# A two-block transformer step in split fp32 on one core: where the second layer's attention units, three norm spreads and the input's transfers stand in the order of work

## The reference, cut to what matters

```python
def rms_norm_2(x, g):
    return x * rsqrt(mean(x * x, axis=-1) + EPS) * g

def first_block(x, c, ...):
    shift, scale, gate = split(silu(c) @ w_mod + b_mod, 3)
    h = rms_norm(x, g_pre) * (1 + scale) + shift
    q, k, v, g_att, u, g_lru, merge = split(h @ w_in)
    ...
    return x + gate * rms_norm(out, g_post)

def second_block(x, c, ctx, ...):
    for l in range(2):
        hx = modulate(rms_norm_2(x, norm1_g[l]), mod_x[0], mod_x[1])
        zx = split(hx @ w_in[l], 10)
        ...
        # y_b: softmax(q1 k1) - lam * softmax(q2 k2), times v, 4 heads,
        #      512 queries over 512 + 256 keys
        x = x + mod_x[2] * (concat([y_a, y_b, y_c, y_d]) @ w_out[l])
        hx = modulate(rms_norm_2(x, norm2_g[l]), mod_x[3], mod_x[4])
        x = x + mod_x[5] * (square(relu(hx @ w1[l])) @ w2[l])
        # l = 0 only: the same for the context
    return rms_norm_2(x, final_g)
```

## Time and profile before

| | |
|---|---|
| median of 3 runs | 2106.29 us (2105.07, 2106.29, 2112.48) |
| profiled execution | 2109.13 us, its span 2107.2 us |
| granted TensorE clock, mean of the span | 0.992 |
| PE busy | 2049.4 us (97%) |
| DVE, ACT, POOL busy | 1271.3, 795.0, 72.4 us |
| DMA | 249.18 MB, mean 118 GB/s |
| largest group | L2005, products of `hxh` with `whi`, 1464 times, 586.4 us |

### The profile page before, as it was taken

The page is one execution under the profiler, slowest core; times in us unless marked ns, Lnnn a source line. Parts: engine busy times, 40 slices in busy tenths (PEclk is TensorE's granted clock), DMA queues, the critical chain, the costliest instruction groups (busy, mean ns, idle before and its releaser), DMA issues.

```text
span 2107.2 us, 26544 instructions
## 1 busy us (share of the span) xinstructions
PE 2049.4 (97%) x11156; PEld 1750.1 (83%) x11156; DVE 1271.3 (60%) x1699; ACT 795.0 (38%) x1126; POOL 72.4 (3%) x81
## 2 busy tenths in 40 slices
PE   6999999999999999999999999999999999999998
PEld 5989888778888988888888888888787788888887
DVE  7467766866757986637446455464687646344343
ACT  4333334584343366434122131122535534132231
POOL 0000000000120000020000000001100010000001
PEclk9999999999999999999999999999999999999999
DMA  8643523524322531123233233232343122222221
GB/s 287 228 157 123 206 94 123 186 98 177 143 100 65 165 98 70 71 92 121 91 110 113 96 134 109 100 120 91 120 148 90 71 90 99 83 99 100 100 98 63
DMA packets 54054, 249.18 MB, mean 118 GB/s; under 512 B 6224, under 2 KB 12512, under 8 KB 35504
## 3 DMA queue, kind: packets, MB, share of 16 engines
q1 hardware_dynamic: 52048, 242.41, 33.3%
q10 hardware_dynamic: 1296, 2.63, 0.4%
q0 software_dynamic: 592, 2.46, 0.3%
HBM read 232.53 MB, written 12.06 MB: 116 GB/s over the span
## 4 chain that ended last, share of the span: by engine, by line
PE 55%; DVE 4%; ACT 1%; issue 1%; DVEq 0%; ACTq 0%
PE banks L2005 51%; DVE small L1390 1%; PE banks L667 1%; ACT prob L996 1%; DVE prob L1410 1%; DVE xT L1536 0%; PE banks L720 0%; PE banks L618 0%; PE banks L619 0%; PE banks L620 0%; PE banks L656 0%; PE banks L1933 0%; PE banks L606 0%; DVE dconv L1374 0%; PE banks L636 0%
## 5 line engine op out<-in xcount | busy, mean ns | idle before, releaser
L2005 PE MATMUL banks<-hxh,whi_f 128*128 128x512 f32 (+1 forms) x1464 | 586.4, 401 | 11.5 <-ACT hxh L2195 7.1
L2005 PE MATMUL banks<-hxh,wlo_f 128*128 128x512 f32 (+1 forms) x1464 | 571.5, 391 | 0.0
L2005 PE MATMUL banks<-hxl,whi_f 128*128 128x512 f32 (+1 forms) x1464 | 556.3, 389 | 0.2 <-DVE hxl L2455 0.2
L2376 DVE TENSOR_TENSOR wlo_f<-raw_f,whi_f 128x2048 fp32r<-128x2048 f32 x130 | 298.1, 2293 | 177.0 <-ACT whi_f L2155 176.8
L2155 ACT ACTIVATE whi_f<-raw_f 128x2048 fp32r<-128x2048 f32 x130 | 247.9, 1907 | 306.2 <-PE banks L2005 288.1
L2005 PEld LDWEIGHTS banks<-hxh,whi_f 128*128 128x128 f32 x1464 | 277.2, 189 | 71.6 <-issue 15.1
L2005 PEld LDWEIGHTS banks<-hxh,wlo_f 128*128 128x128 f32 x1464 | 276.8, 189 | 58.6
L2005 PEld LDWEIGHTS banks<-hxl,whi_f 128*128 128x128 f32 x1464 | 275.7, 189 | 57.2 <-issue 1.9
L2005 PE MATMUL banks<-fxh,whi_f 128*128 128x512 f32 (+1 forms) x528 | 205.4, 389 | 2.2 <-DVE cT L1536 1.1
L2005 PE MATMUL banks<-fxh,wlo_f 128*128 128x512 f32 (+1 forms) x528 | 203.8, 386 | 0.0
L2005 PE MATMUL banks<-fxl,whi_f 128*128 128x512 f32 (+1 forms) x528 | 203.4, 385 | 0.0
(11 more groups left out here) (342 smaller groups left out, 3166.1 us busy)
## 6 DMA issues: line engine op xcount, KB each, us to landing
raw_f<-in_wst SPq DMA_DIRECT2D x133, 1024.0 KB, 4.9
mvr<-in_mst SPq DMA_DIRECT2D x120, 512.0 KB, 5.9
stack<-qk_parts SPq DMA_DIRECT2D x36, 192.0 KB, 6.7
x_kept<-xT SPq DMA_DIRECT2D x2, 2048.0 KB, 8.7
raw_f<-in_wst SPq DMA_DIRECT2D x8, 384.0 KB, 6.5
xT<-x_kept SPq DMA_DIRECT2D x2, 1536.0 KB, 8.7
qk_parts<-qk_h SPq DMA_DIRECT2D x3, 768.0 KB, 3.8
qk_parts<-qk_l SPq DMA_DIRECT2D x3, 768.0 KB, 3.8
```

Of the source, the lines that this page charges most:

```text
L2005: last = pe.matmul(o, (wh, wl)[w][:, k, c, :], r[part][:, k, :], start=(k == order[0] and parts is not LOW and (w, part) == (0, 0)), stop= ...
L2376: dve.tensor_tensor(wlo[r][:], raw[r][:], whi[n % 2 if n > N_FIRST else n][:].bitcast(F32), ALU.subtract).then_inc(w_lo, 1)
```

## The change

Five things, all in order and placement; the arithmetic of the results stays as it was but for the order of the squares' sums.

- `Plan`: l=1's units are all three steps apart, its first scores of both groups are listed two steps sooner (l=0's first scores one), and what follows the first group (`mean`, `sums`, `spread`, `mix`) two steps sooner. The convolution has three taps fewer ahead of the units in l=1 (14 and 13 for 14 and 16) and one fewer in l=0.
- Spreads: `norm_spread` of l=0's second norm stands before the step k=5 of the context's last eight; that of l=1's first norm before the step (1, 2) of the context's last chunk, with the coefficients made ahead of the reciprocal, the last gates copied aside for the residual, and the context's second residual (and its square) made after the fourth tile; the first product of l=1 waits for its banks by another semaphore. The second half's spread stands one piece sooner, and the first block's last spread one step sooner.
- Start: x in four transfers of 512 KB, two on each queue, those of SP ahead of the constants; squares 0, 1, 4, 7 on VectorE and 2, 3, 5, 6 on ScalarE; four sums of pairs, and PE sums each pair, four groups of four products.
- The modulation products ahead of the loop: one before the reciprocal and one after it, where there were three and one.
- Four semaphores become two (mask shares one with x's third piece, the context's c with the fourth).

```diff
         self.u0 = 20 * l
         self.a, self.b = (6, 68) if l == 0 else (6, 65)
-        self.mean, self.sums, self.spread, self.mix = (53, 56, 59, 62) if l == 0 else (46, 51, 55, 59)
-
-        self.slow = (0, 0) if l == 0 else (2, 1)
+        self.early = {0: 1} if l == 0 else {0: 2, self.cut: 2}
+        self.mean, self.sums, self.spread, self.mix = (53, 56, 59, 62) if l == 0 else (44, 49, 53, 57)
     def start(self, v):
-        first, u, slow = (self.a, v, self.slow[0]) if v < self.cut else (self.b, v - self.cut, self.slow[1])
-        return first + 3 * u + min(u, slow)
+        return self.a + 3 * v if v < self.cut else self.b + 3 * (v - self.cut)
     def scores(self, v):
-        return self.start(v) - 3
+        return self.start(v) - 3 - self.early.get(v, 0)
     def turned(self, v):
         return self.start(v) + 2
...
         qk_hi, qk_lo = sem("qk_hi"), sem("qk_lo")
         stored = sem("stored")
-        n_pre, n_post = Norm(SX, True), Norm(SX, False)
+        n_pre, n_post = Norm(SX, True, KT // 2, KT // 2), Norm(SX, False)
         n_mix, n_ff, c_mix, c_ff = [], [], [], []
         for l in range(L2):
...
                 rhs = XC if j in (3, 4) or l == 0 and j > 1 else X
                 if j == 0:
-                    gemm(base, 0, rhs, first=(l == 0), ready=(lambda k: wait_high(SX, n_mix[l], k), lambda k: wait_low(SX, n_mix[l], k)),
+                    gemm(base, 0, rhs, first=(l == 0), bank_free=x_free if l else None, ready=(lambda k: wait_high(SX, n_mix[l], k), lambda k: wait_low(SX, n_mix[l], k)),
                          between={(0, 5): lambda: norm_sums(SC, c_mix[1], nsqm)} if l else {})
                 elif j == 1 and l:
...
                     if k == 4:
                         norm_sums(SX, n_ff[0], nsq2)
+                    if k == 5:
+                        norm_spread(SX, n_ff[0])
                     wait_low(SC, c_ff[0], k)
                     for c in range(2):
                             pe.wait_ge(ctx_free, c + 1)
                         step(n, 0, k, c, C)
-                norm_spread(SX, n_ff[0])
                 for k in range(KT):
                     wait_high(SX, n_ff[0], k)
...
                                     if (c, k) == (1, 0):
                                         norm_sums(SX, n_mix[1], nsq3, 1)
+                                    if (c, k) == (1, 2):
+                                        norm_spread(SX, n_mix[1])
                                     last = step(n, 1, k, c, hid[1:])
                                 last.then_inc(acc_ready[c], 1)
-                            norm_spread(SX, n_mix[1])
                             continue
                         if l and n == base + N_FF - 1:
...
                     act.activation(nsq3[:, 1 if c else KT - 2, :], xT[:, KT - 2 + c, :], ACT.Square).then_inc(SX.squared, 1)
                 norm_root(SX, n_mix[1])
-                for c in range(2):
-                    act.wait_ge(acc_free[c], n + 1)
-                    norm_square(SC, cT, nsqm, KT - 2 + c)
+                act.wait_ge(acc_free[0], n + 1)
+                norm_square(SC, cT, nsqm, KT - 2)
                 act.wait_ge(coefs, 3)
                 for k in range(KT):
                     norm_high(SX, n_mix[1], hxh, k, mod_shift(0, k, 0))
+                    if k == 3:
+                        act.wait_ge(acc_free[1], n + 1)
+                        norm_square(SC, cT, nsqm, KT - 1)
                     if 2 <= k < 6:
                         split_quarter(n + 2, k - 2)
...
                         split(n + 1)
                     low(j - 3)
-                    conv((9, 12)[j - 3] if two else (14, 16)[j - 3])
+                    conv((9, 11)[j - 3] if two else (14, 13)[j - 3])
                 if j < 3:
                     split(n + 2)
...
                             dve.wait_ge(x_part, c + 1)
                             residual(KT - 2 + c, c, 1, (0,), x_free)
+                        g = mod2_0 + 2 * (3 * KT + 2 * KT + KT - 2) + 1
+                        link(dve.tensor_copy(last_gates, small[:, g:g + 3:2]))
+                        coefficients(1)
                         norm_inverse(SX, n_mix[1])
-                        for c in range(2):
+
+                        def last_context(c):
                             dve.wait_ge(acc_ready[c], n + 1)
-                            residual(KT - 2 + c, c, 1, (1,), acc_free[c])
-                        for c in range(2):
-                            dve.wait_ge(acc_free[c], n + 1)
-                        coefficients(1)
-                        modulate(SX, n_mix[1], xT, hxh, hxl, 0, 0)
+                            x_ = cT[:, KT - 2 + c, :]
+                            dve.scalar_tensor_tensor(x_, acc[:, c, T:TX], last_gates[:, c:c + 1], x_, ALU.mult, ALU.add
+                                                     ).then_inc(acc_free[c], 1)
+
+                        last_context(0)
+                        modulate(SX, n_mix[1], xT, hxh, hxl, 0, 0, late={3: lambda: last_context(1)})
                         split_half(n + 2, 0)
                         norm_inverse(SC, c_mix[1])
...
                 f = slice(CW * k, CW * k + CW)
                 sync.dma_start(raw_f[:, :, f], wst[0:N_FIRST, :, f].rearrange("n p f -> p n f")).then_inc(w_first[k % 4], 16)
+            for i in (0, 2):
+                sync.dma_start(xT[:, 2 * i:2 * i + 2, :], xrs[:, 2 * i:2 * i + 2, :]).then_inc(ld_x[i], 16)
             sync.dma_start(consts[:], cst).then_inc(ld_const, 16)
-            sync.dma_start(xT[:, 4:KT, :], xrs[:, 4:KT, :]).then_inc(ld_x[1], 16)
             for k in range(KT):
                 load_mv(2 * k)
...
         @block.tensor
         def _(pe):
-            def gemm(n, s, rhs, first=False, ready=None, between={}, order=tuple(range(KT)), at=None, fill=None):
+            def gemm(n, s, rhs, first=False, ready=None, between={}, order=tuple(range(KT)), at=None, fill=None,
+                     bank_free=None):
...
                     if fill:
                         fill(n, KT * c + k)
-                    if k == order[0] and not first:
+                    if k == order[0] and bank_free:
+                        pe.wait_ge(bank_free, c + 1)
+                    elif k == order[0] and not first:
                         pe.wait_ge(acc_free[c], n if at is None else n - 3 if n < 6 else n - 1)
                 def part(k, c, parts=ALL):
...
                     if i == 2:
                         half_sums(q, sq, 1)
-                    if i == 4:
+                    if i == 3:
                         half_spread(q, 1)
                     r = [(hxh[:, :, columns(h)], hxl[:, :, columns(h)])]
...
                     last.then_inc(acc_ready[c], 1)
             pe.wait_ge(ld_const, 16)
-            norm_sums(SX, n_pre, nsq)
+            for i in range(KT // 2):
+                pe.wait_ge(SX.added, i + 1)
+                for j in range(SX.nj):
+                    last = pe.matmul(SX.st[:, j:j + 1], nsq[:, 2 * i, j * P:(j + 1) * P], ones[:, 0:1],
+                                     start=(i == 0 and j == 0), stop=(i == KT // 2 - 1), skip_group_check=True)
+            last.then_inc(SX.summed, 1)
             norm_spread(SX, n_pre)
             for k in range(KT):
...
                 if s in columns_at:
                     column_sums(columns_at[s])
-                if s == 31:
+                if s == 30:
                     norm_spread(SX, n_mix[0])
                 if j == 0:
...
         def _(act):
             act.dma_start(c1b[:], cbt[0]).then_inc(ld_c1, 16)
-            act.dma_start(xT[:, 0:4, :], xrs[:, 0:4, :]).then_inc(ld_x[0], 16)
+            for i in (1, 3):
+                act.dma_start(xT[:, 2 * i:2 * i + 2, :], xrs[:, 2 * i:2 * i + 2, :]).then_inc(ld_x[i], 16)
             act.dma_start(vecs[:], vec).then_inc(ld_vec, 16)
             def split(n):
...
             act.wait_ge(eps_set, 1)
             act.activation(scr[:, 0:1], epsc, ACT.Sqrt)
-            for k in range(KT):
-                act.wait_ge(ld_x[k // 4], 16)
+            for k in (2, 3, 5, 6):
+                act.wait_ge(ld_x[k // 2], 16)
                 norm_square(SX, xT, nsq, k)
             norm_root(SX, n_pre)
...
                     split(n + 2)
                 if n == 5:
-                    act.wait_ge(ld_c2, 32)
+                    act.wait_ge(ld_x3_c2, 48)
                     act.activation(c2b[:], c2b[:], ACT.Silu).then_inc(silu_c, 1)
             act.wait_ge(at_out, 16)
...
             for c in range(2):
                 dve.memset(lam_p[:, c:c + 1], 0.0).then_inc(f_sq, 1)
+
+            def square(k):
+                dve.wait_ge(ld_x[k // 2], 16)
+                link(dve.tensor_tensor(nsq[:, k, :], xT[:, k, :], xT[:, k, :], ALU.mult))
+
+            def add_pair(i, n):
+
+
+                if n:
+                    dve.wait_ge(SX.squared, n)
+                dve.tensor_tensor(nsq[:, 2 * i, :], nsq[:, 2 * i, :], nsq[:, 2 * i + 1, :], ALU.add).then_inc(SX.added, 1)
+
```

(23 more changed lines are left out.)

13 lines of the change are left out of this document (8 added, 5 removed).

## The result

The changed kernel takes 2087.5 us (median of 5; 2085.54 to 2094.18) against 2106.29; the ratio is 0.9914, 95% interval 0.9900 to 0.9928, so 18.1 us less, between 15.2 and 21.1 (the medians alone differ by 18.8). The forecast was 2086.5, or 19.8 less.

The account below looks back on a forecast made before the run. TensorE bounds the kernel, busy 2049.4 of 2107.2 us; only its idleness and half-clock stretches can be won. Start 3.3, spreads 4.8, units 6.7, 4.0 and .9 sum to 19.7, giving a forecast of 2086.5 us, range 2079 to 2096.

Parts of the forecast that it names:

- Start: First norm: smaller x pieces and shared squares end the sums at 17.7, 3.6 won; VectorE's loop takes back .3: 3.3 us.
- Rival A: The start gains nothing: constants land behind x at 13.9 or later, sums end as before; 2089.9 us, chance .08.
- Spreads: Norm spreads moved ahead of products left, so PE's waits behind them go; four terms, 4.8 us together.
- The fourth: Spread of layer 1's first norm moved sooner: the wait of 2.15 before its product goes, 2.1 us won.
- Rival E: Moved spreads come before their reciprocals, so PE stands there as long as before; 2091.4 us, chance .06.
- Units: Layer 1's two attention groups: three-step spacing and sooner first scores remove waits, 6.7 and 4.0 us.
- The first group: Layer 1's first attention group: scores before values end VectorE's waits and gaps, 8.9 less costs: 6.7 us.
- The split ahead of unit 3's copy: Layer 1's first group: ScalarE's earlier high split holds values(3), costing between 0 and 1.91 us, taken as .8.
- The second group: Layer 1's second attention group: scores(14) before values(12) removes a 2.01 wait and half-rate stretch; 4.0 us.
- Rival B: Half the units' gain goes to another wait, such as the split or a late exponential; 2092.4 us, chance .13.
- C: The units' plan does nothing, each unit being bound by its ring of engines; 2098.2 us, chance .12.
- D: Slower: units packed at three steps make PE wait in each and stay at 1.2 GHz; 2172 us, chance .03.

Follow-up runs that it names:

- run 1: Changed kernel with the constants first on SP's queue again, x's two pieces behind them; 2089.09 us, ratio 0.9923.
- run 8: Changed kernel with the column of ones for the first norm's sums set by VectorE instead of taken from the constants; 2082.32 us, ratio 0.9892.
- run 10: Changed kernel with ScalarE's exponential of layer 1's lambda behind the eviction of the layer's first output tile; 2086.1 us, ratio 0.9900.
- run 2: Changed kernel with two modulation products ahead of the first norm's reciprocal and one behind it; 2089.98 us, ratio 0.9926.
- run 7: Changed kernel with layer 1's convolution taps back at 14 and 16 ahead of the units; 2087.07 us, ratio 0.9914.
- run 6: Changed kernel with the spread of layer 0's second norm one step sooner still, directly behind its column sums; 2086.88 us, ratio 0.9913.
- run 4: Changed kernel with layer 1's intervals of four steps kept, only the first scores two steps sooner; 2097.54 us, ratio 0.9963.
- run 3: Changed kernel with layer 1's first scores back at their old distance, all units three steps apart; 2090.1 us, ratio 0.9930.
- run 9: Changed kernel with ScalarE's copy of a unit's turned tile ahead of the due evictions and high split, both layers; 2087.47 us, ratio 0.9909.
- run 5: Changed kernel with the spread of layer 1's first norm behind all the context's products again; 2088.08 us, ratio 0.9916.
- run 11: Changed kernel with the edits of run 9, run 10 and run 8, and three groups of column sums instead of four; 2085.74 us, ratio 0.9898.
- run 12: The changed kernel again, nothing edited, on the same chip; 2086.91 us, ratio 0.9906.

## Why the prediction was right, and where its terms were not

**What bounds it** held: the gain came from PE's waits and from its stretches at half rate, as the stage table adds up. That the sum came out so near is in part luck. The stages won 22.37 in the traces, the medians differ by 18.8, and the forecast of 19.8 lies between. The terms for half rate were read from one execution, whose clock was at the low end of 22. Stages that no edit touches move by up to 4 us from one program to the next (last section). And terms missed in opposite directions, the start by 0.6 less, one spread by 2.1 more.

**Start, 3.3 against 2.68: mis-sized in its second half.** The constants were ready at 10.40 (I took 10.3) and the sums ended at 17.39 (17.7); before, they ended at 21.13, not at the 21.3 that I took. At the first product the gain was 3.9. I took 0.3 for the loop behind it and it took 1.25: VectorE's rounds are 4.48 long without a wait, two of them waited besides for a modulation tile, 0.33 and 0.49 (runs 1 and 8 show the same), and PE, which had slack at the end before, now waits 0.70 for the seventh `hxh`:

```profile
49.90 0.47 PE L2019 MATMUL banks<-hxh,whi_f 128*128 128x512 f32 x1 [0.70 <-ACT hxh L2215]
```

In the runs with this start unchanged the gain at the loop's end, against the same trace of the kernel before, lay between 2.2 and 3.5, so a miss of 0.6 is not clear of that scatter. That the constants set the start was right as far as it went, but run 1 shows x to be as late; only run 8 won. Rival A fell: the constants came at 10.40 and not at 13.9 or later, and with two more transfers x was complete at 10.69, where the two of 1 MB had it at 10.8. The Trainium skill's rule on transfers of 1 MiB or more ("DMA: Bandwidth & Descriptors", section "Bandwidth") does not decide here; the first quarter was usable sooner, at 5.87.

**Spreads, 4.8 against 6.9.** Three of the four terms were near (0.4, 1.6 and 0.7 against 0.20, 1.83 and 0.73). The fourth, 2.1 against 4.15, was mis-sized: I counted the wait of 2.15 and not what the clock did around it. The windows of the kernel before, which I had not read there:

```profile
1476.00:1482.00 6.00, 6.00 (x40) 6.00 (x41) 0.55 (x2) 0.68 (x2) 0.73 (x1) 0.73 0.00 0
1482.00:1488.00 6.00, 3.85 (x17) 3.15 (x16) 5.27 (x11) 3.00 (x6) 0.00 (x0) 0.78 0.77 209
```

0.27 x 6 = 1.6 was lost at the column sums and about as much, 0.22 x 6 = 1.3 and some more in the next microseconds, behind the wait; against these stands the new wait of 1.35 for the eviction, the stall that is late next, which I did not name. Run 10 shows its price as 1.22. That the changed kernel ran its column sums at 1.00 is not shown to be its doing: with the same code the clock fell there in runs 2 and 7, and the stage was 0.5 longer in both. So about 3.6 of the 4.15 stand without that luck. Rival E fell for the change as made; run 6 shows that one step more would have brought it about.

**Units, 10.7 against 11.59, layer 0's 0.9 against 1.07.** Run 4 gives most of it back, so the three steps, by which the scores come before the values, were the reason; the order by itself was not tried. The first group won 7.40 (I took 6.7). Its sooner first exponentials are worth 0.88 (run 3), near the 0.75 that I took. The split ahead of unit 3's copy, for which I took off 0.8, costs PE 1.31 but the group only 0.12 (run 9); the 0.7 between is what the group won beyond its forecast. The second group won 4.19 (4.0). The path differs from mine, though: in the first group I summed VectorE's idle times. On PE the waits for exponentials stayed at 6.2 in both groups together, and what it won was 3.7 of waiting for turned tiles and, by the estimate above, 8.3 of clock. Rival B and C fell by the stage table, D by the clock of 1.00; run 4 shows a part of D: where waits of about 2 us return, one of four lowers the clock. What the Trainium skill says of a wait in every tile and each next tile cold ("TensorE: Matmul & The Clock Gate", section "HAM oscillation — how this bites in real kernels") agrees here with the row at 1657.85 and not with the longer wait at 1611.38.

## What to carry to other kernels

Where a fixed order of instructions on one engine puts a consumer's late work ahead of a producer's early work, exchange the two before spacing them out; here closer spacing and the order that came with it were worth 7.6 us together, and which of the two did it was not parted. Price an exposed wait by the windows around it as well as by its own length, since half rate behind it can double it, and look at more than one execution, since that half rate comes and goes. A wait that goes can be worth its full length (the eviction, 1.22 of 1.35) or almost nothing (the copy, 0.12 of 1.31): look whether the engine that sets the pace stood still for it.

## What the runs showed of the hardware that I had not expected

The length of PE's wait alone did not tell whether the clock falls. Behind waits of 1.86, 2.45 and 2.01 in the kernel before and of 2.03 in run 4 the granted clock was 0.51 to 0.54; behind 1.86, 1.96 and 2.45 in run 4 and 1.75 in run 5 it stayed at 1.00. Behind unit 3's copy, a wait of 1.31 in the changed kernel and of 1.32 in run 1 with the same code, it was 1.00 in the one and 0.54 in the other, where the group took 1.6 longer. The waits of the kernel before at 1.86 and 2.45, then the one of run 1 with its window:

```profile
1579.42 1.55 PE L667 MATMUL banks<-vnat,ptd 128*128 128x64 f32 x12 [1.86 <-ACT ptd L1023]
...
1620.68 0.51 PE L636 MATMUL banks<-stack 128*128 128x512 f32 x1 [2.45 <-ACT prob L996]
...
1579.05 1.81 PE L668 MATMUL banks<-vnat,ptd 128*128 128x64 f32 x12 [1.32 <-ACT ptd L1026]
...
1580.00:1583.75 3.75, 3.75 (x17) 3.32 (x17) 3.44 (x5) 1.59 (x6) 0.00 (x0) 0.54 0.63 138
```

And it fell without any wait to speak of, behind the one-column sums of a norm. At layer 1's first norm it was 0.72 to 0.73 over 6 us in the kernel before and in runs 5, 7 and 11, fell in run 2 too (0.86 over 12 us), and was 1.00 in the changed kernel and the other runs. At the end of the first block (604 to 614), whose code no experiment edits, it was 0.83 in the kernel before, the changed kernel and runs 4 to 7, 10 and 12, and 1.00 in runs 1, 2, 3, 8, 9 and 11, whose first block, behind the start, is shorter by 1.2 to 1.7 than the changed kernel's. In layer 0's units it was 0.51 from 814 to 820.75 in run 10 alone. What decides that is open.

The feed-forward of layer 0, some 520 us that no edit here touches, was up to 2.9 us longer (run 2) and 4.0 shorter (run 6) than in the changed kernel, at a granted clock of 1.00, while the same program run again (run 12) agreed within 0.01. So an edit elsewhere can move it; why was not tried.
